# Opening the even layer in two token parts, with the norm's sums taken from rows that hold tokens on partitions

## The reference, cut to what matters

```
def rmsnorm(x, g):
    y = x * lax.rsqrt(jnp.mean(x * x, axis=-1, keepdims=True) + EPS)
    return y * g

# even layer
xn = rmsnorm(x, g_mix[0])
proj = xn @ w_in            # (1024 -> 2560): q | k | v | xb | gb, each 512 wide
q, k = rmsnorm(q, gq), rmsnorm(k, gk)      # per head of 64
o_a = stick_breaking_attention(q, k, v)
o_b = rg_lru(causal_conv4(xb)) * gelu(gb)
x = x + concat(o_a, o_b) @ w_out
```

## Time and profile before

| | before |
|---|---|
| runs | 2511.43, 2510.85, 2508.8 us; median 2510.85 |
| the profiled execution | 2509.27 us, its span 2507.6 us |
| PE busy | 2451.6 us, 98% of the span |
| DVE, ACT, POOL busy | 70%, 46%, 38% |
| first matmul of a projection | 23.95 us |
| slab x done, slab q begins | 36.48 us |
| key chunk 1 begins | 60.75 us |

### The profile page before, as it was taken

One profiled execution on the slowest core, in us unless ns is written; L12 is line 12 of the kernel. 1 busy time (PEld: TensorE's weight loads), 2 busy tenths in 40 slices (PEclk: granted clock), 3 DMA queues, 4 the chain that ended last, 5 costly groups with the idle time before them and its releaser, 6 DMA issues.

```text
span 2507.6 us, 46213 instructions
## 1 busy us (share of the span) xinstructions
PE 2451.6 (98%) x18709; PEld 2354.5 (94%) x18709; DVE 1754.0 (70%) x2158; ACT 1148.3 (46%) x1849; POOL 947.7 (38%) x617
## 2 busy tenths in 40 slices
PE   7999998899999999999999999999999999999999
PEld 7888786679999999999999999999999999999999
DVE  7456566644978686879888444547878787788885
ACT  5565757542644444444334533525544444453332
POOL 3134343214354545453222411243454545443221
PEclk9999999999999999999999999999999999999999
DMA  5101115852232323238443111122232323266432
GB/s 188 53 28 52 37 35 183 307 176 100 77 110 77 110 79 112 83 109 290 159 145 96 43 52 41 39 91 86 83 114 82 114 82 114 82 227 230 143 104 85
DMA packets 214177, 276.99 MB, mean 110 GB/s; under 512 B 11437, under 2 KB 158998, under 8 KB 210894
## 3 DMA queue, kind: packets, MB, share of 16 engines
q1 hardware_dynamic: 212910, 271.83, 32.1%
q10 hardware_dynamic: 576, 2.10, 0.2%
q0 software_dynamic: 480, 0.11, 0.0%
HBM read 203.57 MB, written 70.43 MB: 109 GB/s over the span
## 4 chain that ended last, share of the span: by engine, by line
PE 71%; DVE 6%; issue 1%; ACT 1%; DMA 0%; ACTq 0%; DVEq 0%; SPq 0%
PE psum_all L2210 54%; PE psum_all L2942 7%; PE psum_all L153 7%; DVE psum_all L2153 1%; PE psum_all L2994 1%; DVE down_x_ffn L2168 1%; DVE x_residual L2548 1%; PE psum_all L3028 0%; PE psum_all L2958 0%; DVE x_residual L2533 0%; DVE ffn_x L2482 0%; DVE blocks L2157 0%; PE psum_all L2982 0%; PE psum_all L2783 0%; ACT ffn_x L2376 0%
## 5 line engine op out<-in xcount | busy, mean ns | idle before, releaser
L2210 PE MATMUL psum_all<-ffn_x,blocks 128*128 128x272 f32 x5760 | 732.3, 288 | 7.1 <-DVE x_residual L2533 5.3
L2210 PEld LDWEIGHTS psum_all<-ffn_x,blocks 128*128 128x128 f32 x5760 | 725.8, 188 | 8.7 <-issue 7.7
L2210 PE MATMUL psum_all<-down_x_ffn,blocks_down 128*128 128x272 f32 x2880 | 369.0, 288 | 2.2 <-DVE x_residual L2599 2.0
L2210 PEld LDWEIGHTS psum_all<-down_x_ffn,blocks_down 128*128 128x128 f32 x2880 | 363.3, 188 | 3.7 <-issue 3.3
L2324 ACT COPY x_residual<-psum_all 128x544 f32<-128x544 f32 x192 | 117.9, 614 | 358.9 <-PE psum_all L2210 358.9
L113 POOL TENSOR_TENSOR w_lo_part<-w_raw,w_hi_part 128x1024 fp32r<-128x1024 f32 x52 | 125.8, 2419 | 353.9 <-ACT w_hi_part L97 353.9
L2599 DVE TENSOR_TENSOR x_residual<-x_residual,psum_all 128x544 f32<-128x544 f32 (+1 forms) x224 | 178.4, 797 | 88.2 <-PE psum_all L2210 84.6
L2163 POOL TENSOR_TENSOR x_residual<-x_residual,rms_scale 128x1088 f32<-128x1088 f32 x48 | 151.6, 3160 | 155.7 <-ACT x_residual L2358 144.9
L2548 DVE SCALAR_TENSOR_TENSOR x_residual<-x_residual,ffn_params 128x1088 f32<-128x1088 f32 x96 | 209.6, 2184 | 0.1
L2533 DVE TENSOR_TENSOR x_residual<-x_residual,psum_all 128x544 f32<-128x544 f32 x144 | 130.2, 904 | 87.8 <-PE psum_all L2210 85.7
L2157 DVE TENSOR_TENSOR blocks<-psum_all,blocks 128x512 fp32r<-128x512 f32 x144 | 99.2, 689 | 115.7 <-ACT blocks L2303 115.7
(11 more groups left out here) (360 smaller groups left out, 4622.7 us busy)
## 6 DMA issues: line engine op xcount, KB each, us to landing
staging_ffn<-hidden_spill SPq DMA_DIRECT2D x54, 816.0 KB, 5.2
hidden_spill<-x_residual SPq DMA_DIRECT2D x24, 1088.0 KB, 4.0
w_raw<-in_w_gate_dram SPq DMA_DIRECT2D x24, 1024.0 KB, 5.4
x_residual<-in_w_up_dram SPq DMA_DIRECT2D x24, 1024.0 KB, 5.2
pages<-in_cache_k_dram SPq DMA_DIRECT2D x64, 256.0 KB, 4.6
pages<-in_cache_v_dram SPq DMA_DIRECT2D x64, 256.0 KB, 5.4
x_spill<-x_residual SPq DMA_DIRECT2D x24, 546.0 KB, 5.2
x_residual<-x_spill SPq DMA_DIRECT2D x24, 546.0 KB, 5.8
```

Source lines behind the costliest of these rows:

```text
L2210: mm = pe.matmul(self.core.ps[:, b + h, 0:HB], wt[:, q * P:(q + 1) * P], xt[:, q, HB * h:HB * (h + 1)], start=first and at == 0, stop=at = ...
```

## The change: what it does

- The row tiles lie in buffers that the layer uses later (`mix`, `take_all`), so they stay readable; the small rows lie in `vtok[0]`.
- DMA order: the gain rows `g_mix` go from GpSimd's queue to SP's, behind tile 0; slab 0 goes from SP's queue to ScalarE's, behind tile 1; slab 2 is loaded before the spill.
- PSUM ring of four banks for the transposed groups in place of six. ScalarE copies groups 0, 2, 4, 6, 8, 9, 10, 12, 14, 15, 16; VectorE 1, 3, 5, 7, 11, 13, 17.
- The hi and lo parts of x are made in two column parts, 0 to 384 and 384 to 1092. The first is made and multiplied by slab 0 while later tiles come: `first_chunk` (hi*hi, hi*lo) after tile 3 and after tile 4, `first_rest` (lo*hi, when the slab's remainder is there) after tile 5. Tiles 6 to 8 and the small rows follow on TensorE, then `first_slab` for chunks 1 and 2.
- The norm's sums: each row tile is squared with an accumulated sum per partition, tiles 0 to 3 and 8 on ScalarE, 4 to 7 on VectorE. ScalarE takes the roots of the 128 x 9 sums, spreads them as nine diagonal matrices (identity times root), and TensorE multiplies these by ones (`rows_pe`), at the place of `sums_pe`; three copies fill `rms_scale`.
- 20 filler transposes stand at the start, the others are gone.

```diff
@@ class Load
+    DVE_GROUPS = (1, 3, 5, 7, 11, 13, 17)
+    RING = (3, 4, 5, 6)
...
     def sync(self, sp):
         self.x_rows(sp, 0)
-        w.load(sp, 0, 0, square_slab(w_in, 1536))
+        sp.dma_start(self.prow[0:16, :], self.core.dram["g_mix"]...).then_inc(self.gains_in, 16)
         for t in (2, 4, 6, 8):
             self.x_rows(sp, t)
         w.load(sp, 1, 1, square_slab(w_in, 0))
...
-    def tensor(self, pe):
+    def tensor(self, pe, first_chunk, first_rest):
         pe.wait_ge(self.const_ready, 4)
-        for n, (t, g) in enumerate(self.groups):
-            ...
-        core.keep_busy(pe, 16)
+        core.keep_busy(pe, 20, core.ps[:, 2, 256:384])
+        self.turn(pe, 0)
+        pe.wait_ge(self.gains_in, 16)
+        pe.transpose(core.ps[:, 7, 224:240], self.prow[0:16, :], core.ident[0:16, 0:16]).then_inc(self.gains_tr, 1)
+        for t in (1, 2, 3):
+            self.turn(pe, t)
+        first_chunk(range(0, 4))
+        self.turn(pe, 4)
+        first_chunk(range(4, KT))
+        self.turn(pe, 5)
+        first_rest()
+        for t in (6, 7, 8):
+            self.turn(pe, t)
+        self.small(pe)
+        self.wait_all_copied(pe)
...
-    def scalar(self, act):
-        for t in (1, 3, 5, 7):
+    def scalar(self, act, norm):
+        self.x_rows(act, 1)
+        w.load(act, 0, 0, square_slab(self.core.dram["w_in_even"][0], 1536))
+        for t in (3, 5, 7):
             self.x_rows(act, t)
+        act.preload_act_table_set("natural_log_exp_and_others")
+        copies(0, 2, 4)
+        w.split_hi(act, 0, 0, 0)
+        act.wait_ge(self.small_copied, 1)
+        self.wait_copied(act, 4)
+        norm.split_act(act, 0, range(0, 4))
+        copies(6)
+        self.wait_copied(act, 5)
+        norm.split_act(act, 0, range(4, KT))
+        copies(8, 9, 10, 12, 14, 15, 16)
+        act.wait_ge(self.pad_ready, 3)
+        self.wait_all_copied(act)
+        norm.split_act(act, 1, range(0, 2))
+        w.split_hi(act, 1, 0, 1)
+        norm.split_act(act, 1, range(2, KT))
+        for i, t in enumerate((0, 1, 2, 3, 8)):
+            norm.square_act(act, i, t, self.row_tiles[t])
+        self.exp_act(act)
+        norm.roots_act(act)
...
+    def vector(self, dve, norm):
+        copies(1, 3, 5)
+        norm.split_dve(dve, 0, range(0, 4))
+        copies(7)
+        norm.split_dve(dve, 0, range(4, KT))
+        copies(11, 13, 17)
+        self.wait_all_copied(dve)
+        norm.split_dve(dve, 1, range(0, KT))
+        ... (three small copies)
+        for i, t in enumerate((4, 5, 6, 7)):
+            norm.square_dve(dve, i, t, self.row_tiles[t])
@@ class Norm
+    PARTS = ((0, 384), (384, T))
+    def square_act(self, act, i, t, rows):
+        act.activation(self.junk[0][0:n, 0:D], rows, ACT.Square, accum_out=self.sums[0:n, t:t + 1]
+                       ).then_inc(self.act_squared, 1)
+    def square_dve(self, dve, i, t, rows):
+        dve.scalar_tensor_tensor(self.junk[1][:, 0:D], rows, 1.0, rows, ALU.mult, ALU.mult,
+                                 accum_out=self.sums[:, t:t + 1]).then_inc(self.dve_squared, 1)
     def roots_act(self, act):
+        act.activation(self.roots, self.sums, ACT.Ln, scale=1.0 / D, bias=EPS).then_inc(self.s_root, 1)
+        act.activation(self.roots, self.roots, ACT.Exp, scale=-0.5).then_inc(self.s_root, 1)
+        for t in range(9):
+            act.activation(self.diagonals[:, t * P:(t + 1) * P], self.core.ident[:, :], ACT.Copy,
+                           scale=self.roots[:, t:t + 1]).then_inc(self.s_diagonal, 1)
+        for c, (a, b) in enumerate(CUT_USED):
+            act.wait_ge(self.s_mm, c + 1)
+            act.copy(self.core.rb[:, a:b], self.core.ps[:, 6 + c % 2, 0:b - a]).then_inc(self.s_rb, 1)
+    def rows_pe(self, pe):
+        for c, (a, b) in enumerate(CUT_USED):
+            pe.wait_ge(self.s_diagonal, 3 * c + 3)
+            ... (ones x diagonals[:, a:b]; the third also waits for s_rb 1)
@@ phase_even
         def _(sp):
             intake.sync(sp)
+            w.load(sp, 2, 0, square_slab(w_in, column["k"]))
+            intake.wait_all_copied(sp)
...
+            def first_chunk(steps):
+                pe.wait_ge(w.s_hi, 1)
+                for k in steps:
+                    pe.wait_ge(norm.s_lo, k + 1)
+                    for xt in (act_hi, act_lo):
+                        pe.matmul(bank(("x", 0, 0), 0, CUT[0][1]), w.hi[:, 0, k * P:(k + 1) * P],
+                                  xt[:, k, 0:CUT[0][1]], start=k == 0 and xt is act_hi, stop=False)
+            def first_rest():
+                w.wait_ready(pe, 0)
+                ... (lo of the slab x act_hi, 8 matmuls)
             def first_slab():
                 for k in range(KT):
-                    pe.wait_ge(norm.s_lo, k + 1)
+                    pe.wait_ge(norm.s_lo, KT + k + 1)
-                        for c, (a, b) in enumerate(CUT_USED):
+                        for c in (1, 2):
```

More of the change, by code:

```diff
@@ L237, in x_rows, with wait_copied, wait_all_copied @@
+    def wait_copied(self, eng, n):
+        by_dve = sum(m <= n for m in self.DVE_GROUPS)
+        if n in self.DVE_GROUPS:
+            eng.wait_ge(self.dve_copied, by_dve)
+        else:
+            eng.wait_ge(self.act_copied, n + 1 - by_dve)
+    def wait_all_copied(self, eng):
+        eng.wait_ge(self.act_copied, len(self.groups) - len(self.DVE_GROUPS))
+        eng.wait_ge(self.dve_copied, len(self.DVE_GROUPS))
     def x_rows(self, eng, t):
-        dr, xs = self.core.dram, self.xs
+        dr = self.core.dram
@@ L410, with __init__ @@
 class Norm:
-    def __init__(self, core, ctx, tag, act_hi, act_lo, sums, squares, gain):
-        self.core, self.hi, self.lo, self.sums, self.sq, self.gain = core, act_hi, act_lo, sums, squares, gain
+    PARTS = ((0, 384), (384, T))
+    def __init__(self, core, tag, act_hi, act_lo, sums, roots, diagonals, junk, gain):
+        self.core, self.hi, self.lo, self.sums, self.roots = core, act_hi, act_lo, sums, roots
+        self.diagonals, self.junk, self.gain = diagonals, junk, gain
         def sem(name):
@@ L449, in sums_pe @@
[L449 to L467 removed]
+        self.s_hi, self.s_lo, self.act_squared, self.dve_squared = (sem(n) for n in (
+            "xn_hi", "xn_lo", "act_squared", "dve_squared"))
@@ new lines, in __init__, with split_act, split_dve @@
+        self.s_root, self.s_diagonal, self.s_mm, self.s_rb = (sem(n) for n in (
+            "roots", "diagonals", "rows_mm", "rb_ready"))
+    def split_act(self, act, part, steps):
+        a, b = self.PARTS[part]
+        for k in steps:
+            act.activation(self.hi[:, k, a:b], self.core.x[:, k, a:b], ACT.Copy,
+                           scale=self.gain(k)).then_inc(self.s_hi, 1)
+    def split_dve(self, dve, part, steps):
+        a, b = self.PARTS[part]
+        for k in steps:
+            dve.wait_ge(self.s_hi, KT * part + k + 1)
+            dve.scalar_tensor_tensor(self.lo[:, k, a:b], self.core.x[:, k, a:b], self.gain(k),
+                                     self.hi[:, k, a:b].bitcast(F32), ALU.mult, ALU.subtract).then_inc(self.s_lo, 1)
@@ new lines, in rows_pe @@
+    def rows_pe(self, pe):
+        for c, (a, b) in enumerate(CUT_USED):
+            pe.wait_ge(self.s_diagonal, 3 * c + 3)
+            out = self.core.ps[:, 6 + c % 2, :]
+            if c < 2:
+                mm = pe.matmul(out[:, 0:b - a], self.core.ones[:, :], self.diagonals[:, a:b], start=True, stop=True)
+            else:
+                pe.wait_ge(self.s_rb, 1)
+                pe.matmul(out[:, 0:SEQ - a], self.core.ones[:, :], self.diagonals[:, a:SEQ], start=True, stop=True)
+                mm = pe.matmul(out[:, SEQ - a:b - a], self.core.ones[0:NS, :], self.diagonals[0:NS, SEQ:b],
+                               start=True, stop=True)
+            mm.then_inc(self.s_mm, 1)
@@ L810, in _ @@
             for j in range(4):
-                for kind in "kvg":
+                for kind in "kvg" if j else "vg":
                     slab(kind, j)
@@ L1122, in cached_finish @@
                 mm.then_inc(fin_done, 1)
-            intake.tensor(pe)
+            intake.tensor(pe, first_chunk, first_rest)
             first_slab()
```

196 lines of the change are left out of this document (83 added, 113 removed).

## The result

The changed kernel took 2515.12 us (median of 12 runs, 2511.99 to 2519.22); the kernel before, beside it, 2510.82 (12 runs, 2507.15 to 2516.87). The ratio is 1.0019, with a 95% interval of 1.0012 to 1.0026: slower by 0.19%, which is 4.3 us, and the interval leaves no change out. I had forecast 2510.7, a shift of -0.2 us. The time lies in the range, near its upper end, but I had forecast next to no change, and what came is a clear loss, towards rival B. The profiled execution took 2518.69 us, its span is 2516.8.

The account below looks back on a forecast made before the run. TensorE, busy 98% of the span, was taken as the bound. Shifts of +3.2 us at slab x's end, +1.6 at key chunk 0 and -0.2 at key chunk 1 gave 2510.7 us, range 2506.0 to 2515.5.

Parts of the forecast that it names:

- rival B: Opening: TensorE stays at 1.2 GHz from 15.3 us; key chunk 1 at 66, +5.6 us, 2516.5; chance 0.08.
- rival A: Opening: VectorE's remainders run beside GpSimd's, so the early part pays; -4.1 us, 2506.8; chance 0.15.
- the waits of 1.1 and 0.6 us: TensorE's waits for ScalarE and VectorE between 44 and 60 us, forecast to be gone.
- part 3: Slab x's remaining 708 columns: ends at 39.7 us, 3.2 later than before, with 2.1 us of TensorE idle at group 2.
- part 2: First chunk of 384 columns: GpSimd's slab 0 remainder stalls VectorE, 0.8 us added for clock, last copy at 28.0.
- -0.2 at k 1: First matmul of key chunk 1 at 60.55 us against 60.75, carried to the end one for one.
- the early part: Multiplying a third of slab x while rows arrive; slab x still forecast to end 3.2 us later.
- my two signs of being wrong: Last copy before 25 or after 31 us, or a shift at key chunk 1 that isn't the end's.
- the list of what would show it: Trace milestones: slab 0 at 13 to 14, last copy near 28, slab x's end near 39.7, key chunk 1 near 60.5.

Follow-up runs that it names:

- e10: Changed kernel, with GpSimd's remainder of slab 0 waiting for VectorE's eight remainders of the first chunk: 2512.59 us, ratio 1.0013.
- e1_fill: Changed kernel plus 40 filler transposes on TensorE between tiles 2 and 3 and 20 behind the small rows: 2511.63 us, ratio 1.0002.
- e4: Kernel before without its 16 filler transposes ahead of the first slab: 2511.51 us, ratio 1.0001.
- e3: Changed kernel with 40 and 20 fillers, and slab 1's upper part made behind all eight upper parts of the 708 columns: 2507.98 us, ratio 0.9987.
- e6: Changed kernel with slab 0 halved over two queues, slab 1's upper part late and 20 fillers behind the small rows: 2513.14 us, ratio 1.0014.
- e8: Kernel before with only the new norm's sums; old intake, DMA order, fillers and single column part: 2506.85 us, ratio 0.9987.
- e9: e8 plus slab 1's GpSimd remainder behind the eighth remainder of x, slab 2 loaded and cut earlier: 2506.68 us, ratio 0.9986.
- e11: Changed kernel with fillers, slab 1's upper part late and slab 0's remainder behind the first chunk's eight: 2506.87 us, ratio 0.9991.
- e12: e11 with slab 0 first on ScalarE's queue, ahead of tile 1, and 36 fillers between tiles 0 and 1: 2505.91 us, ratio 0.9987.
- e2: Changed kernel with slab 1's upper part made on ScalarE behind all eight upper parts of the 708 columns: 2514.68 us, ratio 1.0012.
- e5: Changed kernel with slab 0 loaded in two halves, one on SP's queue and one on ScalarE's: 2513.87 us, ratio 1.0013.
- e7: Changed kernel with slab 0 back on SP's queue, behind the gain rows and ahead of tile 2: 2516.01 us, ratio 1.0028.

## Why the prediction was wrong

**What held.** The order of work at every step; slab 0 landed at 14.2 and tile 3 at 15.6 (forecast 13.3 and 15.3, bound 14.7; issued at 1.2 and 1.7 us):

```profile
w_raw<-in_w_in_even_dram ACTq DMA_DIRECT2D x1, 512.0 KB, 13.0
...
mixed_even<-in_x_prompt_dram ACTq DMA_DIRECT2D x1, 512.0 KB, 13.9
```

VectorE was locked out once at each of GpSimd's first two remainders, 2.27 and 2.42 us (the Trainium skill, "SBUF — State Buffer", "Who interferes with whom", says so, and the trace agrees; rival A, the other reading, is out by e10). The last copy ended at 29.06 (28.0). From slab x's end on the forecast's own steps were right to 0.6 us: it ended at 42.74 (39.7), the sums began at 51.12 (48.1), k 0 at 57.66 (54.1), k 1 at 63.86 (60.55), late by 3.0, 3.0, 3.6 and 3.3; the waits of 1.1 and 0.6 us are gone. Small prices were right or near: a square with its sum 1.21 us on VectorE with 0.07 more for reading the sum out (I took 1.4), 1.06 and 0.19 on ScalarE, nine diagonals 2.75 us (2.7):

```profile
37.52 1.06 ACT L505 ACTIVATE squares_then_scale<-mixed_even 128x1024 f32<-128x1024 f32 x1
38.48 0.19 ACT L505 ACTIVATION_READ_ACCUMULATOR squares_then_scale<-mixed_even 128x1 f32 x1
39.66 1.21 DVE L511 SCALAR_TENSOR_TENSOR xb_padded<-mixed_even 128x1024 f32<-128x1024 f32 x1
40.80 0.07 DVE L511 DVE_READ_ACCUMULATOR xb_padded<-mixed_even 128x1 f32 x1
45.57 2.75 ACT L523 ACTIVATE v_tokens_pair<-identity,k_rows_out 128x128 f32<-128x128 f32 x9
```

**The step that failed** is the clock term of part 3: there was none. I had added 0.8 us for the clock in part 2 and taken the 708 columns at full speed, "groups 2 to 7: 33.9 + 5.8 = 39.7". Measured, the six groups from 35.07 to 42.74 took 7.7 us instead of 5.8, since TensorE ran them at half the clock until about 39.0. The other part of the miss is a size: the remainder of group 2 came at 35.0, 1.1 us late, nearly all of it the last copy's lateness, and that begins with slab 0, whose landing at 14.2 made its upper part ready at 15.3 (14.4) and VectorE's first four remainders at 19.8 (18.8). The two make 3.0 of the 3.3 us by which k 1 missed; the second wasn't tested by an experiment of its own. e1_fill measures the first by itself: with the clock at 1.00 in that stretch k 1 comes 1.73 us earlier. That the clock fell there and not in before is seen in what TensorE did: before, 16 fillers ran in the time to the first matmul of slab x and left a wait of 1.20 us; in the change the small transposes (8, 24 and 74 columns wide) and a wait of 1.89 us stood there. e4 shows the converse. And all kernels agree: in the eight with fillers ahead of slab x's main part the granted clock from 24 to 36.5 us is 1.00 (before, e1, e3, e6, e8, e9, e11, e12), in the six without it is 0.79 to 0.90 (after, e2, e4, e5, e7, e10).

**My rival B** had the right place in the argument and too small a chance, 0.08: it asked for slow work past 24 us and gave k 1 at 66. The clock was slow from about 11.9 to 22.0 us, recovered, and was slow again from 32.3 to 39.0. I had set against it that before was fast within 4 us of its start, and that the Trainium skill ("TensorE: Matmul & The Clock Gate", "What you observe") sees the same of a steady stream. Here TensorE worked from 15.70 on with only 0.7 us of waiting, and was fast only at 22.0; the trace doesn't agree with the 4 us for a stream that a wait breaks up. And neither the row nor the page spoke of the second fall, which I didn't look for: wherever fillers were taken away, the next dense stretch was to be priced at both levels.

**The other side of the sum, "-0.2 at k 1".** I had two large terms that cancelled, and e8 measures them: the sums -3.55, the early part +6.66. From my own steps the sums were worth about -3.4 (+3.2 at slab x's end became -0.2), so that size was right. The early part was priced at +3.2 and cost 6.7 at k 1. What it could bring, a third of slab x done while rows arrive, was lost to four things that runs take away, and a fifth that none does. Step by step at k 1, in one profiled execution each: the slow clock in the 708 columns (e1 against the change, 1.73), slab 1's remainder on GpSimd and what hangs on it (e3 against e1, 1.92), slab 0's remainder (e11 against e3, 0.22), slab 0 behind tile 1 (e12 against e11, 1.29, with the fillers at another place), and the last that is left, 1.50 (58.70 against 57.20): e12 still has its last copy at 26.98 where e8 has it at 20.94. The copies share VectorE and ScalarE with the parts of x of the first chunk, and up to 1.0 us of it may be the wait for slab 0's remainder that e12 itself brought; neither was tested.

**The criterion.** Neither of my two signs of being wrong was met: the last copy came between 25 and 31, and the shift at the end (the median moved by 4.3 us, by its interval 3.0 to 6.5) holds the shift at k 1, +3.1. The signs were too weak, and the time lay in the range only because the range reached to B's edge, 2515.5; what tells me wrong is k 1 itself, +3.1 where I had said -0.2 (60.5 on the list of what would show it, 63.86 measured). Some slips in the working changed nothing: 12.5 us over 8 groups is 1.57 and not 1.49, but the 0.97 us for six matmuls held (0.96 to 0.97 at full clock), and rival B's own sum gives +5.4 and not +5.6. The profiled execution is 9.4 us longer than that of before; only 3.1 of these stand at k 1, and behind it what follows took 2452.9 us instead of 2446.9.

**What stays open.** Behind k 1 the traces took between 2444.0 us (e12) and 2456.6 (e4), with one to four more stretches of half clock at places that differ from run to run, so a single profile says nothing to 5 us about the end. Whether the changed opening makes such stretches more frequent can be read from the mean granted clock of every execution. It is 0.9948 on average over the 12 executions of the changed kernel and 0.9976 to 0.9978 over the 33 to 35 of the kernel before in each of the later rounds. The difference is worth about 7 us of full clock. The opening alone, in the one profiled execution, lacks 8.7 us of it up to 62 us (a clock of 0.86, where before has 1.00):

```profile
0.00:62.00 62.00, 49.88 (x279) 46.13 (x280) 36.56 (x77) 32.82 (x58) 19.74 (x38) 0.86 0.56 190
```

So the opening's two slow stretches are enough, and on average the later ones are not more frequent. What isn't settled is why the order of the medians isn't that of k 1: kernels with fillers in the wait for rows (e1, e3, e11, e12) have ratios from 0.9987 to 1.0002, all others with the two-part opening (after, e2, e5, e6, e7, e10) from 1.0012 to 1.0028, although e6 and e10 reach k 1 at 61.31 and 61.17, earlier than e1 at 62.13. The clocks of all executions give a hint: the profiled ones of e6 and e10 had 0.997, the other ten of each 0.9954 and 0.9956 on average, so the profiled ones were better than most of their kind. Over all executions the first four have 0.9966 to 0.9977 and the other six 0.9948 to 0.9957. That the slow stretches of the intake are longer in most executions than in the profiled one would explain it; where in those executions the clock was low no run here shows.

## What to carry to other kernels

When an edit moves or removes filler work on TensorE, price every dense stretch behind the new waits at both clock levels, not only the first one, and look for the fall in the durations of single instructions. When two parts of a change cancel in the forecast, the sum is as uncertain as each of them: here the one part alone (e8) gave a time that the measurement doesn't tell from that of the best mended version of both (2506.85 and 2505.91). And before a late stage is called cheap, ask what hides it (in the old kernel softplus on VectorE hid a slab that ended 1.7 us late, e4); a part of the same change may take the cover away, as the new sums took softplus's away.

## What the runs showed of the hardware

- The place on the queue counted for more than the size: slab 0 of 512 KB took 13.0 us behind tile 1, 10.4 behind tile 0 and the gain rows (e7), the half of it on the same queue 10.4 as well (e5), and 5.4 when it was the first on its queue (e12). What stood behind it was late too: tile 2 landed at 14.0 in e5, tile 3 at 15.6 in the change. By what rule the two queues share isn't shown; the two theories tried (e5 and e7, e12) both missed.
- The exclusion of VectorE and GpSimd works both ways: 0.62 against 2.27 us for VectorE (e10, after), and 3.33 against 2.4 for GpSimd (e9).
- The accumulated sum of an instruction is read out by an instruction of its own, 0.07 us on VectorE and 0.19 on ScalarE.
- TensorE fell to half its clock (0.79 us for a pair of matmuls, 0.49 later) about a microsecond after dense work had begun behind a wait of 1.89 us, and stayed there for 6.7 us of matmuls with one wait of 0.66 us among them. With fillers in that wait it didn't fall in any profiled execution.
- The granted clock can read 1.00 while the first work is slow: in the kernel before sixteen transposes took 3.65 us and later 1.97, at a granted clock of 1.00 in both.
